# Summing the modulation chains as a moving operand, and pooling on VectorE, in a two-block transformer kernel

## The reference

```python
mod = silu(c) @ ada_w[i] + ada_b[i]         # 1024 -> 6*1024, for each of 4 layers
sh1, sc1, gt1, sh2, sc2, gt2 = split(mod, 6)
h = rms_norm(x, g) * (1 + sc1) + sh1
...
# layer 0 mixes by pooling (half of the features) and attention (the other half)
for gi, w in enumerate((2, 4, 8, 16)):      # 128 features each
    mean = (cs[hi] - cs[lo]) / (hi - lo)    # mean over a window of w tokens
    outs.append((mean - u[gi]) @ pool_w[gi])
y = concat(pool, attention(q, k, v)) @ w_out
```

## Time and profile before

| | |
|---|---|
| runs of the kernel before (3) | 2556.5 us median, 2555.28 to 2557.27 |
| the profiled execution, its own time | 2558.39 us |
| its span, first to last instruction | 2556.6 us |
| mean granted TensorE clock | 0.961 of full speed |
| TensorE busy | 2362.8 us, 92% |
| VectorE busy | 1715.2 us, 67% |
| ScalarE busy | 1020.0 us, 40% |
| GpSimd busy | 67.1 us, 3% |

### The profile page before, as it was taken

The page is one execution under the profiler, slowest core; times in us unless marked ns, Lnnn a source line. Parts: engine busy times, 40 slices in busy tenths (PEclk is TensorE's granted clock), DMA queues, the critical chain, the costliest instruction groups (busy, mean ns, idle before and its releaser), DMA issues.

```text
span 2556.6 us, 46809 instructions
## 1 busy us (share of the span) xinstructions
PE 2362.8 (92%) x20170; PEld 1952.1 (76%) x20170; DVE 1715.2 (67%) x3302; ACT 1020.0 (40%) x1893; POOL 67.1 (3%) x70
## 2 busy tenths in 40 slices
PE   6899989999998999999999889898989989998997
PEld 5675467888875578889887789894777888677886
DVE  5966779677646247887763777756356865745576
ACT  2225243323322224544432453334245653644465
POOL 0300000000000000000000000020000011000000
PEclk9899989999998999999999999899899999997999
DMA  7330426665542100000003577550056943003574
GB/s 310 133 131 1 158 106 222 230 256 216 213 155 75 57 1 3 3 4 3 11 4 118 200 273 294 188 182 1 9 206 230 345 165 132 1 1 132 181 303 191
DMA packets 47279, 348.02 MB, mean 136 GB/s; under 512 B 5248, under 2 KB 5248, under 8 KB 5728
## 3 DMA queue, kind: packets, MB, share of 16 engines
q1 hardware_dynamic: 45936, 334.52, 35.1%
q0 software_dynamic: 1136, 10.51, 1.0%
HBM read 343.96 MB, written 1.05 MB: 135 GB/s over the span
## 4 chain that ended last, share of the span: by engine, by line
PE 76%; DVE 16%; ACT 6%; issue 2%; DMA 1%; DVEq 0%; ACTq 0%; POOLq 0%
PE banks L537 23%; PE banks L932 9%; PE banks L1852 6%; DVE arena L616 3%; PE banks L2708 3%; PE banks L2709 3%; PE banks L2710 3%; PE banks L786 2%; PE banks L1718 2%; PE banks L1034 2%; PE banks L1013 2%; PE banks L1929 1%; PE banks L2739 1%; PE banks L2741 1%; PE banks L2740 1%
## 5 line engine op out<-in xcount | busy, mean ns | idle before, releaser
L616 DVE SCALAR_TENSOR_TENSOR arena<-weight_slots,silu_c,arena 128x256 f32<-128x256 f32 x776 | 328.1, 492 | 0.0
L515 DVE TENSOR_TENSOR moe_w_low<-weight_slots,moe_w_high 128x2048 fp32r<-128x2048 f32 x96 | 217.9, 2289 | 70.4 <-ACT moe_w_high L506 69.5
L932 PE MATMUL banks<-arena,weight_slots 128*128 128x256 f32 (+1 forms) x768 | 229.6, 457 | 13.5 <-DVE arena L1599 11.7
L932 PEld LDWEIGHTS banks<-arena,weight_slots 128*128 128x128 f32 x768 | 148.3, 194 | 88.7 <-issue 73.6
L506 ACT ACTIVATE mlp_w_high<-weight_slots 128x2048 fp32r<-128x2048 f32 x64 | 122.3, 1911 | 178.3 <-PE banks L537 105.4
L506 ACT ACTIVATE moe_w_high<-weight_slots 128x2048 fp32r<-128x2048 f32 x96 | 181.2, 1911 | 23.8 <-PE banks L2741 19.7
L515 DVE TENSOR_TENSOR mlp_w_low<-weight_slots,mlp_w_high 128x2048 fp32r<-128x2048 f32 x64 | 146.3, 2286 | 49.2 <-ACT mlp_w_high L506 49.1
L1852 PE MATMUL banks<-weight_slots,arena 64*64 64x64 f32 (+1 forms) x3648 | 147.0, 223 | 18.9 <-ACT arena L1872 13.3
L1852 PEld LDWEIGHTS banks<-weight_slots,arena 64*64 64x64 f32 x3648 | 138.9, 135 | 27.2 <-ACT arena L1872 15.2
L2708 PE MATMUL banks<-moe_w_high,slots_x 128*128 128x512 f32 x320 | 133.2, 416 | 11.8 <-DVE moe_w_low L515 11.8
L2709 PE MATMUL banks<-moe_w_low,slots_x 128*128 128x512 f32 x320 | 129.2, 404 | 0.0
(11 more groups left out here) (392 smaller groups left out, 5196.6 us busy)
## 6 DMA issues: line engine op xcount, KB each, us to landing
weight_slots<-weights SPq DMA_DIRECT2D x318, 1024.0 KB, 4.8
arena<-small POOLq DMA_DIRECT2D x1, 2560.0 KB, 9.0
arena<-x_t POOLq DMA_DIRECT2D x1, 2048.0 KB, 15.9
arena<-bias POOLq DMA_DIRECT2D x1, 2048.0 KB, 9.5
constants<-consts POOLq DMA_DIRECT2D x1, 1410.0 KB, 21.2
out_t<-arena SPq DMA_DIRECT2D x1, 1024.0 KB, 3.9
parameters<-params POOLq DMA_DIRECT2D x1, 775.0 KB, 9.2
arena<-pool_inv POOLq DMA_DIRECT2D x1, 512.0 KB, 10.4
```

The costliest lines, as they stand in the source:

```text
L515: nc.vector.tensor_tensor(self.pair(j)[1], slot(j, 0, SLOT), self.pair(j)[0], ALU.subtract).then_inc(*v.step("used", j))
L616: nc.vector.scalar_tensor_tensor(a_, w, c, a_, ALU.mult, ALU.add).then_inc(*v.step())
L932: ins = nc.tensor.matmul(psum(b, 0, w), slot(j, k, 256, i * P, P), moving(k), start=(k == 0), stop=(k == KT - 1))
```

## The change

1. The chains from mod0 block 8 on and all of mod1 to mod3 are summed the other way round. The stationary operand is a 128 x 24 matrix whose column n is ones and all others zeros (cut out of 47 new columns of constants), the moving operand is the accumulator, 256 columns for each vector. The sums of block n come out in row n of bank 7; all chains of a layer add into the same 24 rows.
2. When a layer's 24 rows are complete VectorE copies them to SBUF (`mod_rows_vector`), over the last chain's accumulator, TensorE turns them with 4 transposes (two vectors) or 2 (one vector) back into bank 7 (`mod_turn`), and `mod_vectors` reads the turned sums. The chain that would take that accumulator next waits for the turn.
3. The order of the blocks is changed in the MLP of layer 0: the mod1 blocks end one projection block earlier, and the mod2 blocks begin one later.
4. The pooling instructions leave GpSimd's queue. VectorE runs the same 18, one after each unit 2 to 13 of LAT and 2 to 7 of CON. Only the clearing of the pads stays on GpSimd.

```diff
-    order += mixed(("mlp1_0", 4), ("mod1", 7)) + mixed(("mlp2_0", 4), ("mod1", 7))
-    order += (mixed(("mlp1_0", 4), ("mod2", 6)) + mixed(("mlp2_0", 4), ("mod2", 6))) * 2
+    order += mixed(("mlp1_0", 4), ("mod1", 8)) + mixed(("mlp2_0", 3), ("mod1", 6)) + ["mlp2_0"]
+    order += ["mlp1_0"] + mixed(("mlp1_0", 3), ("mod2", 6)) + mixed(("mlp2_0", 4), ("mod2", 6))
+    order += mixed(("mlp1_0", 4), ("mod2", 6)) + mixed(("mlp2_0", 4), ("mod2", 6))
...
+                m_, n_ = v.chained[v.chains - slots]
+                v.wait_ge(*(after("mod_turned", m_) if n_ == 23 else after("mod_summed", m_, n_)))
...
+        def mod_row(pe, m, n):
+            mod_bank(pe, m, part_of(m))
+            pe.wait_ge(*after("mod_acc", m, n))
+            acc = chain_sums[m, n]
+            pe.wait_ge(*after("consts"))
+            vecs = mod_vecs(m, n)
+            for a_, s in enumerate(vecs):
+                ins = nc.tensor.matmul(psum(7, s * 256, 256, ROWS_24), cn("one_row", 23 - n, 24), acc[:, a_],
+                                       start=(n == first_row(m) and a_ == 0), stop=True, skip_group_check=True)
+            ins.then_inc(*pe.step("mod_summed", m, n))
+
+        def mod_rows_vector(v, m):
+            v.stage("mod")
+            v.wait_ge(*after("mod_summed", m, 23))
+            at_ = 256 * mod_vecs(m, first_row(m))[0]
+            nc.vector.tensor_copy(rows_of(m)[:, at_:512], psum(7, at_, 512 - at_, ROWS_24)).then_inc(*v.step("mod_rows", m))
+
+        def mod_turn(pe, m):
+            pe.wait_ge(*after("mod_rows", m))
+            for s in mod_vecs(m, first_row(m)):
+                for i in range(2):
+                    ins = nc.tensor.transpose(psum(7, (2 * s + i) * 24, 24), rows_of(m)[:, s * 256 + i * P:s * 256 + i * P + P],
+                                              cn("ident", 0, 24, ROWS_24))
+            ins.then_inc(*pe.step("mod_turned", m))
...
                            then=y_sums(pe, "x01", BOTH, lambda: side_blocks(pe, block_of["mlp1_0"][0], 0)))
+            mod_turn(pe, 0)
             x_sums_tensor(pe, "n2_0", [X, CTX])
...
+                        if q % 2 and g == KT - 2:
+                            mod_turn(pe, 1 + q // 2)
...
+                if n % 16 == 15:
+                    mod_rows_vector(v, 1 + n // 16)
+                    v.stage("mlp0" if n == 15 else "mlp0b")
                 MLP0.low(v, n + MLP0.ahead)
...
+            side_blocks(pe, block_of["ev2_in"][0], 0)
+            mod_turn(pe, 3)
             for g in range(KT - 2, KT):
                 sums_tensor(pe, "y_x12", ONE, g)
-            side_blocks(pe, block_of["ev2_in"][0], 0)
...
-            att_vector(v, LAT)
-            att_vector(v, CON)
+            pooling = pool_steps()
+            def pool_next(n):
+                for _ in range(n):
+                    pool_vector(v, *pooling.pop(0))
+            att_vector(v, LAT, {i: lambda: pool_next(1) for i in range(2, 14)})
+            att_vector(v, CON, {i: lambda: pool_next(1) for i in range(2, 8)})
             v.stage("norm")
             MLP0.low(v, 0)
             MLP0.low(v, 1)
+            mod_rows_vector(v, 0)
             mod_vectors(v, 0, range(2, 6))
```

More of the change, by code:

```diff
@@ L662, in mod_vectors @@
             v.stage("mod")
-            v.wait_ge(*after("mod_summed", m, 4 * chunks[-1] + 3))
+            rows = in_rows(m, 4 * chunks[0])
+            v.wait_ge(*(after("mod_turned", m) if rows else after("mod_summed", m, 4 * chunks[-1] + 3)))
             v.wait_ge(*after("params"))
@@ L674, in mod_vectors @@
                 gains[4] = (pr("norm2_g2", (m - 2) * KT, KT), 1.0)
-            for chunk in chunks:
+            for s in (mod_vecs(m, 4 * chunks[0]) if rows else ()):
+                n0, n1 = 4 * chunks[0], max(n for n in range(24) if s in mod_vecs(m, n)) + 1
+                part = M[:, 2 * n0:2 * n1, s].rearrange("p (n i) -> p i n", i=2)
+                b = bias_at[:, 2 * n0:2 * n1].rearrange("p (n i) -> p i n", i=2)
+                got = psum(7, 48 * s, 48).rearrange("p (i n) -> p i n", i=2)[:, :, n0:n1]
+                nc.vector.tensor_tensor(part, got, b, ALU.add).then_inc(*v.step())
+            for chunk in (() if rows else chunks):
                 vecs = mod_vecs(m, 4 * chunk)
@@ L989, in fill_ready @@
             if held is not None and held[0] == "mod":
-                pe.wait_ge(*after("taken", "mod", held[1], 2 if held[1] == 0 else 0))
+                pe.wait_ge(*after("taken", *held))
             elif held is not None:
@@ L1209, in load_low_rank, with pool_pads, pool_steps @@
             g.eng.dma_start(SORT, small[:, 6656:6656 + N_SORT]).then_inc(*g.step("sorting", by=16, sem="sorting_loaded"))
[L1211 removed]
+        def pool_pads(g):
             g.stage("pooling")
             nc.gpsimd.memset(UP, 0.0).then_inc(*g.step("pads"))
[L1215 to L1228 removed]
+        def pool_steps():
+            return [(gi, lv) for gi in range(4) for lv in range(gi + 3)]
@@ new lines, in pool_vector @@
+        def pool_vector(v, gi, lv):
+            u = UP[:, gi]
+            src = u if lv == 0 else PT3[:, (lv - 1) % 2]
+            if (gi, lv) == (0, 0):
+                v.wait_ge(*after("taken", "ev_in", 3))
+                v.wait_ge(*after("pool_inv"))
+            v.wait_ge(*v.own)
+            if lv <= gi:
+                up, down = (0, 1) if lv == 0 else (1 << (lv - 1), 1 << (lv - 1))
+                lo, hi = 1 << lv, 288 - (1 << lv)
+                nc.vector.tensor_tensor(PT3[:, lv % 2][:, :, lo:hi], src[:, :, lo + up:hi + up],
+                                        src[:, :, lo - down:hi - down], ALU.add).then_inc(*v.step())
+            elif lv == gi + 1:
@@ L1560, in mlp_split_vector @@
             side_chains(v, block_of["ev2_in"][0])
+            mod_rows_vector(v, 3)
+            v.stage("mlp_down")
             EV2.low(v, 0)
@@ L2651, in moe_tensor @@
             held = bank_state["holder"][7]
-            pe.wait_ge(*after("taken", *((*held[:2], 2 if held[1] == 0 else 0) if held[0] == "mod" else held)))
+            pe.wait_ge(*after("taken", *held))
             def unread(n):
```

50 lines of the change are left out of this document (23 added, 27 removed).

## The result

The changed kernel takes 2561.76 us (median of 14 runs, 2556.41 to 2563.23), the kernel before 2556.27 (14 runs, 2554.39 to 2557.56): a ratio of 1.002, 95% interval 1.0012 to 1.0028. The forecast was 2543.1, in a range of 2538 to 2551. It missed by 18.7 us.

A forecast was written before the change was run, and what follows sets the result against it. TensorE, busy 92% of the span, was taken as the full engine. The terms -12.0 + 2.2 - 2.5 + 1.2 - 1.1 - 1.2 = -13.4 took 2556.5 to 2543.1 us, range 2538 to 2551.

The forecast's parts named there:

- Part 1: ev_in: with pooling off GpSimd, chain m10 on VectorE is no longer slowed and TensorE's stall behind e3 goes; -12.0 us.
- e3: A block of TensorE's work in ev_in, not a run; it began at 103.05 and ended at 114.07, before the stall.
- e7: A later block of TensorE's work in ev_in, not a run; forecast to start at 152.6 where it started at 164.64.
- m10: A chain on VectorE in ev_in, slowed beside GpSimd's pooling; forecast to take about 6.2 us instead of 21.6.
- m9: A chain in ev_in before m10; its sum ends as e3 begins at 103.05 and frees the accumulator the chain after m10 needs.
- Part 2: LAT and CON: pooling in VectorE's queue lengthens ten LAT units and is free in CON's waits; +2.2 us.
- Part 3: MLP of layer 0, ev_in, ev_out: turned-round sums cost 0.43 us a vector, and are hidden in layer 1; -2.5 us.
- Part 4: Turns of the summed rows: +1.2 us in the MLPs, -1.1 after ev_out, with squares at full clock.
- Part 5: MLP of layer 0: the new block order removes TensorE's 1.24 us wait on `mod_vectors`; -1.2 us.
- rival (d): LAT and CON: TensorE, waiting in each unit, falls to the lower clock; up to 32 us, net 2573; chance 0.03.

The follow-up runs named there:

- late pooling: Changed kernel with 128-column row sums and the 18 pooling instructions behind units 10 to 13 of LAT and 2 to 15 of CON: 2550.59 us.

## Why the prediction was wrong

- **Part 1 (-12.0) was right,** mechanism and size: with this part alone 110.7 to 98.8, all of it between e3 and e7 (-11.9). That the changed kernel's stage shows -11.7 is partly luck: between e3 and e7 it gained 10.9, as four groups of row sums took 1.0 back, and 0.8 came from a shorter stretch at the lower clock where ev_in begins. Chain m10 takes 6.2, and the wait for m9's accumulator is hidden, as worked out. The rule of the Trainium skill that the part cited (page "GPSIMD Engine Reference", section "Key points") agrees with the trace: 21.6 us for the chain beside GpSimd's instructions, 6.2 without them.
- **Part 2 (+2.2) was right:** 2.6 at equal clock, units of 2.90, instructions of 0.69, CON free.
- **Part 3 (-2.5) is the step that failed,** in sign and in size. It priced a row sum by the rate of matmuls that follow others of their own form, 0.43 for a vector, and that rate is right inside a group (the 2.77 for twelve records after ev_out is 0.23 a record). What it left out is the step between the forms. The text named it, "if switching to the narrow operand costs what it saves", and then bounded it at 0 without a row; the cost is 0.28 net per group, and the sums of the first MLP come to +6.9 on TensorE's account (+5.6 where they are not hidden behind ScalarE) instead of -2.2. The second half of the error is the sentence that in layer 1 the sums are hidden. That holds in mlp1, where TensorE waits for low parts. In mlp2 it waits only at the first of the 12 groups, and the other 11 at 0.29 are 3.2 of the 4.0 that this stage is longer.
- **A row that speaks of it stood in the trace of before.** The values of the attention have a stationary operand of 64 columns. There too the load starts with its matmul, and the load of the next 128-column form as well:

```profile
218.84 0.85 PEld L1034 LDWEIGHTS banks<-arena 128*64 128x64 f32 x8 [0.29 <-ACT arena L1135]
218.84 1.09 PE L1034 MATMUL banks<-arena 128*64 128x128 f32 x8
...
222.51 0.42 PEld L1023 LDWEIGHTS banks<-constants,arena 128*128 128x128 f32 x4 [0.17 <-issue]
222.51 0.66 PE L1023 MATMUL banks<-constants,arena 128*128 128x128 f32 x4
```

- **And a rule.** The Trainium skill, page "TensorEngine Tiling (Array Packing)", section "Key Properties", says that changing the tiling mode drains TensorE, and its section "Overview" lists a free or contraction dimension of 64 or less as the case for splitting the array into such tiles. The row sums agree with both: 64 columns cost as 24, 96 as 128. The page gives no size; here it is 0.32 us for in and out. That an operand of 64 columns or less puts the array into such a mode is a reading, not shown: the traces show only that the loads are no longer ahead. And it doesn't fit every row. In the trace of before, 32 steps go from a transpose with 15 columns (L1023, the first at 2172.76) to one with 128, and there the load is 0.12 ahead as between equal forms. So the rule of 64 is shown here for these row sums, not for every narrow operand.
- **Part 4 was right in size, and partly by luck.** It is -1.1 after ev_out to the digit, but the gain is the clock's and not the turning's: the squares stand at half rate or near it in three of the four kernels with the sums in columns (3.62, 3.58, 3.12) and at full rate in the fourth (1.96), and against that one the turned sums are 0.6 slower there. In all ten kernels with row sums the squares run at full rate, so the sums may well bear on it; that the one-column records alone bring the lower clock is refuted. Besides, the narrow groups of the same stage took 1.2 of it back (93.6 against 92.3 with 96 or 128 columns); the turn of four takes 0.42, and 0.35 to the next product. **Part 5** was right in its mechanism, the wait of 1.24 is gone.
- The first MLP then comes to +6.9 for the sums, -1.3 for the three groups hidden behind ScalarE's high parts, +1.0 for its turns and -1.5 for the wait (in the kernel before 565.48 - 559.87 - 3.62, less the sum's 0.50): +5.1, measured +5.3. With 128 columns the sums come to 2 x 1.8 + 17 x 0.91 + 6 x 0.46 = 21.8, 8.0 less; only 0.3 of them is hidden, which leaves 7.0, and 7.0 is what the stage is shorter with idle matmuls (396.0 against 403.1). Without them it is 8.0 (395.0 against 403.0); the 1.0 more lies in the first 110 us of the stage, most of which VectorE paces.
- **The clock cost what rival (d) named, in another way.** The sum had it at nothing, in LAT and in the causal attention. That rival had LAT's many small waits bring the lower level, up to 32 us. What happened is that the stretch behind the one wait of 3.1 us, present before too, became 13.6 us long instead of 6.8: 5.2 - 2.6 = 2.6 us. This wait brings the stretch: with idle matmuls in it, the windows stand at 1.00 in both kernels. The profiles read the same way give 6.8 us in the three kernels with the pooling on GpSimd and no idle matmuls, and with it on VectorE 13.6 in five, 10.2 and 6.8 in one each. So the pooling's place seems to bear on it, and not by the time at which its instructions run, since late pooling had 13.6 too. Why was not settled.
- **Open:** the low stretch of 10.2 us in the causal attention. It costs 3.7 of the 4.5 us between the spans, yet the instructions and waits ahead of it are those of the kernel before. Idle matmuls were not tried at that place. The row sums are not cleared of it either: the attention of layer 2 takes 147.0 or 147.1 us in all four kernels with the sums in columns, without a low stretch, and 149.5 to 151.1 in nine of the ten with row sums, each with a low stretch of 3.4 to 10.2 us; only the one with 64 columns takes 147.2. With one trace of each kernel, why is not shown.

Between the spans the forecast was -13.4 and the result +4.5, 17.9 us apart. The step between forms explains 7.8 in the first MLP (5.6 + 2.2), 3.2 in layer 1, 1.0 in ev_in and 1.2 after ev_out: 13.2. The clock explains 2.6 in LAT and 3.7 in the causal attention, less the 0.8 where ev_in begins: 5.5. That is 18.7, and small terms of both signs are left, the largest of them 2.5 less in the recurrent layer and mlp1 of layer 1. Of that, 1.4 is in mlp1, which takes 114.6 in all four kernels with the sums in columns and 113.1 to 113.2 in all ten with row sums; so there the turned sums gained something that the prediction had at nothing. No experiment followed it.

## What to carry to other kernels

Before giving TensorE a smaller operand, look in the trace for a step between forms, and compare the start of the weight load with that of its matmul there; a few small matmuls that stand alone between full-width ones can be cheaper with a stationary operand padded to over 64 columns, even with columns of no use. A gain on an engine that stalls another can be worked out from the trace to a few tenths; price the edits that ride along with it just as hard, for here they, together with the clock, ate all of it. And where a stage begins with a wait of some us on TensorE, it is worth filling: three idle matmuls gained 2.0, 4.6 and 5.5 us in that stage of three kernels (3.9, 7.7 and 6.8 between the medians).

## What was not expected of the hardware

- A group of row sums costs 0.32 us more with a stationary operand of 24 or 64 columns (1.23 and 1.24 for two vectors, 0.78 and 0.81 for one) than with 96 or 128 (0.91, 0.46). Within a group nothing is lost.
- One column as moving operand, with 128 x 128 of data as weights, costs as much as the reverse: 0.95 against 0.91 for two vectors. Eight records of one column take as long as four of 256.
- One TensorE wait of 3.1 us was followed by 6.8 to 13.6 us at 1.2 GHz, in the same place, and by none when 2.8 us of it were filled. Where the stretch falls elsewhere differs between kernels with the same work in front of it in the stage. Single runs of one kernel differ by up to 10 us (128 columns with late pooling, 2542.1 to 2552.2), and the granted clock goes with it: of the changed kernel with idle matmuls, six runs at 0.967 or 0.968 took 2552.4 to 2554.1, five at 0.964 or 0.965 2557.5 to 2559.2. Medians of five runs that differ by less say little here, and the stages' durations say more.
